# Differential softmax attention beside gated linear attention: finished output tiles copied out of PSUM by ScalarE, and key, weight and input splits reordered

## The chip, the core and the metric

The kernel runs on one core of one Trainium2 chip, as one program. The metric is the device time of an execution in microseconds (us). Engines are called TensorE (PE in the profile; its weight loads are PEld), VectorE (DVE), ScalarE (ACT), GpSimd (POOL) and SyncE (SP, which here only issues transfers).

## What is computed

Two transformer blocks over 1024 tokens of 1024 channels, in fp32. The change lies in the first block's mixer. It has two attentions, whose outputs are joined and multiplied with `w_out`:

```python
o_a = rms_norm(o_fwd + o_bwd) * silu(r_g)            # gated linear attention, 4 heads, both directions
lam = exp(sum(q1*k1)) - exp(sum(q2*k2)) + lambda_init
o_b = diff_attention(qd, kd, vd, positions, rel_bias_table, lam)   # softmax(q1 k1 + bias) - lam * softmax(q2 k2 + bias), times v
o_b = rms_norm(o_b, diff_norm_w) * (1 - lambda_init)  # 4 heads of 128
x = x + g_a * (concatenate([o_a, o_b]) @ w_out)
```

## The kernel before

TensorE multiplies fp32 values as sums of two rounded parts, a high one (`hi`) and a low one (`lo` = value - `hi`): three products, hi*hi, hi*lo and lo*hi. Who makes the two parts is named all through the program: the high part is a copy into the rounded type, the low part a subtraction.

`both_attentions` is one block of the program with an instruction list for each engine. Engines run their lists in order and meet at semaphores.

**Linear part** (`gla_mixer`, about 342 to 393 us). 16 steps, two of them a batch. For step n TensorE makes `scores(n+1)`, `turn` of an older batch on every second step, and `outputs(n)`. ScalarE squares a finished pair of outputs (L2629; the squares themselves are thrown away, into the weight buffer `w_staged`) and takes the root; VectorE masks, carries the states on, scales and gates. `outputs` of a later batch waits for the gate of the one that used its PSUM pair before. After batch 4, ScalarE calls `when_half`, which rounds the keys of head 0.

**Softmax part** (about 388 to 554 us). N = 32 tiles: 4 heads by 8 tiles of 128 queries, each against all 1024 keys. Tile n goes through these steps:

- GpSimd prepares the tile's queries and their two parts (L3070 to L3075). In `KEYS` stands after which tiles it also splits the keys of a head (L3059, L3061); at tiles 8 and 9 it makes the low parts of the two first strips of `w_out` (L3081).
- TensorE: `scores(n)` (L3098), two maps of 128x1024, both softmaxes of the difference.
- VectorE: `add_bias(n)` (L3201, two instructions), then `join(n)` (L3206 to L3212), which subtracts the two maps in the ratio of their sums.
- ScalarE: two `exp` (L3175).
- TensorE: `turn(n)` (L3107), eight transposes of the joined map into PSUM.
- ScalarE: `take_turned(n)` (L3147), copies them to `att_aT`.
- TensorE: `multiply(n)` (L3116), eight products with the values into one of two PSUM places `ps_o[n % 2]`.
- VectorE: `take(n)` (L3217), copies the finished 128x128 output to `att_o`.
- ScalarE: `square(n)` (L3153), for the RMS norm.

The order on each engine is written by hand, as iterations n: TensorE does `scores(n+1)`, `multiply(n-2)`, `turn(n-1)`; VectorE `add_bias(n)`, `take(n-3)`, `join(n-1)`; ScalarE two `exp` of tile n, `take_turned(n-1)`, `square(n-4)`. The waits at the products are these:

```python
def multiply(n):
    h = n // TT
    pe.wait_ge(copied, n + 1)      # take_turned(n)
    if n:
        pe.wait_ge(taken, n)       # take(n - 1)
```

After the last tiles come the norm's factors (`mean`, `root`, `factor`), and for each head `scale` (VectorE, L3242), `turn_head` (TensorE, L3124) and `place` (ScalarE, L3161), which put the head into `mixed`. Then semaphores are cleared, all engines meet at a barrier, and `project("mix")` multiplies `mixed` with `w_out`. There `SplitParts` splits the eight input rows of `mixed`: ScalarE the high parts (L1567 for two halves of row 0, L1571 for the others), VectorE the low ones (L1582, L1586); TensorE's products (L348) follow row by row. The strips of `w_out` for it come through `w_staged`, two of them loaded and split during the softmax part.

Of the kernel before, what the change touches and what calls it, by code (L numbers as in the profile page):

```python
# [20 lines left out]
P = 128  # L21
# [1532 lines left out]
class SplitParts(Part):  # L1554


    def __init__(self, nc, nm, x, kb, hi, lo, halved=False, open_gate=None):
        self.open_gate = open_gate
        self.nc, self.nm, self.x, self.kb, self.hi, self.lo = nc, nm, x, kb, hi, lo
        self.split0, self.half0, self.halved = nm.n_split, nm.n_half_split, halved  # L1560
        nm.n_half_split += halved
# [15 lines left out]
    def vector(self, dve, behind_first=None):  # L1577
        if self.halved:
            for a, ready, at, done in ((0, self.nm.half_high, self.half0 + 1, self.nm.half_split),
                                       (BANK, self.nm.hi_ready, self.split0 + 1, self.nm.split)):  # L1580
                dve.wait_ge(ready, at)
                self.nc.vector.tensor_tensor(self.lo[:, 0, a:a + BANK], self.x[:, 0, a:a + BANK], self.hi[:, 0, a:a + BANK].bitcast(F32),  # L1582
                                             ALU.subtract).then_inc(done, 1)
        for k in range(self.halved, self.kb):
# [990 lines left out]
def gla_mixer(nc, g, ctx, mixed, kd, vtok, qk, fwd, kst_tok, first, psum, junk, att, o_n):  # L2575
# [46 lines left out]
    def scalar(act, when_half):  # L2622
# [13 lines left out]
        for b in range(BATCH):  # L2636
# [3 lines left out]
            if b == BATCH // 2:  # L2640
                when_half(act)
# [7 lines left out]
    def tensor(pe, ahead):  # L2649
# [321 lines left out]
def both_attentions(nc, g, st, mixed, kd, vtok, lam, image_stored, qk, fwd, kst_tok, first, qk_at, fwd_at, q_room_at, states_at):  # L2971
# [5 lines left out]
    KEYS = {0: 0, 3: 1, 5: 2, 7: 3}  # L2977
    base, loads = st.strips, tuple(st.loads)
    with ExitStack() as ctx:
# [9 lines left out]
        junk_of_linear = st.staged[1][:, 0:4 * P].rearrange("p (n c) -> p n c", c=P)  # L2989
        k_rooms = [(qk_at, qk_at + 2 * ROW), (qk_at + ROW, qk_at + 3 * ROW), (fwd_at + ROW, fwd_at + 3 * ROW), (parts_at, parts_at + ROW)]  # L2990
# [7 lines left out]
        e = [[fwd[:, 0, :], fwd[:, 2, :]], [later[:, i, :] for i in range(2)]]  # L2998
        a = [over(f"att_a{s}", [P, L], states_at + s * ROW) for s in range(2)]
        aT = [over(f"att_aT{s}", [P, TT, P], states_at + (2 + s) * ROW) for s in range(2)]  # L3000
        o = over("att_o", [P, N, P], states_at + 4 * ROW)
# [6 lines left out]
        of_linear = gla_mixer(nc, g, ctx, mixed, kd, vtok, qk, fwd, kst_tok, first, psum, junk_of_linear, att, o_n)  # L3008
# [35 lines left out]
        def _(sp):  # L3044
            linear_sync(sp)
            sp.wait_ge(image_stored, 16 * TT * HEADS)
            rows = g.dram["bias"].rearrange("h r k -> (h r) k")
            for n in range(N):
# [3 lines left out]
                if 2 <= n < 4:  # L3052
                    sp.dma_start(st.staged[n - 2][:, :], g.dram["w_out"][n - 2]).then_inc(st.loaded[n - 2], 16)

        @block.gpsimd
        def _(pool):
            def split_keys(h):
                if h:
                    nc.gpsimd.tensor_copy(kd_hi[h][:, :], kd[:, h, :]).then_inc(k_high, 1)  # L3059
# [3 lines left out]
            linear_gpsimd(pool)  # L3063
            linear_loaded(pool)
            linear_updated(pool)
            for n in range(N):
# [10 lines left out]
                if n in KEYS:  # L3077
                    split_keys(KEYS[n])
                if 8 <= n < 10:
                    pool.wait_ge(st.hi_ready, base + n - 7)  # L3080
                    nc.gpsimd.tensor_tensor(st.lo[n - 8][:, :], st.staged[n - 8][:, :], st.hi[n - 8][:, :].bitcast(F32),  # L3081
                                            ALU.subtract).then_inc(st.split, 1)
# [59 lines left out]
        def _(act):  # L3142
# [5 lines left out]

            def square(n):
# [44 lines left out]
        def _(dve):  # L3194
# [20 lines left out]
            def take(n):  # L3215
                dve.wait_ge(summed, n + 1)
# [2464 lines left out]
```

## Time and profile before

| | |
|---|---|
| time, median of 3 executions | 2237.03 us (2232.4 to 2237.46) |
| profiled execution: its time, its span | 2236.17 us, 2234.3 us |
| mean granted clock of TensorE | 0.985 of full speed |
| TensorE busy | 2134.9 us, 96% of the span |
| VectorE busy | 1569.6 us, 70% |
| ScalarE, GpSimd busy | 813.6 us, 36%; 944.4 us, 42% |

The span goes from the first to the last instruction; the profiled execution's own time has 1.9 us around it. Busy times are of the whole program; the change touches the part from 342 to about 580 us, so the table only says that TensorE leads.

### The profile page before, as it was taken

To read this page: it belongs to the slowest core of one execution; us is meant where nothing else is said; L and a number is where in the kernel's file an instruction comes from. 1 tells how busy PE (TensorE), PEld (TensorE's weight loads), DVE (VectorE), ACT (ScalarE), POOL (GpSimd) and SP (SyncE) were. 2 spreads that over 40 slices of the span, in tenths; PEclk is the share of its full clock that TensorE was granted. 3 is DMA by queue.
4 is the path that set the end of the run, shared out by engine and by line. 5 is a ranking of instruction groups with operands and counts; after the bars stand their busy time and mean duration, and the time that the engine had idled before them with its cause. 6 is when DMAs were issued, how large, how long until landed. Compare 5 with 4: busy or idle time off the path is not lost. (4 is left out here: it accounts for less than half of the span.)

```text
span 2234.3 us, 29465 instructions
## 1 busy us (share of the span) xinstructions
PE 2134.9 (96%) x11276; PEld 1735.6 (78%) x11276; DVE 1569.6 (70%) x2298; ACT 813.6 (36%) x1132; POOL 944.4 (42%) x719
## 2 busy tenths in 40 slices
PE   6999999898999999999999999999997999999997
PEld 4887887687877788888777786888877787777876
DVE  5785516997858888888778776869986636764344
ACT  4104432687234344434322224115225323442331
POOL 0222342631435888888656455111000021798710
PEclk9999999999999999999999999899998999999998
DMA  7595732332432333333577764494458323111131
GB/s 275 213 335 162 204 122 96 123 120 69 150 117 76 122 131 131 109 128 110 209 244 244 247 211 169 157 300 132 141 174 288 125 87 118 48 48 48 57 132 75
DMA packets 155431, 337.74 MB, mean 151 GB/s; under 512 B 14039, under 2 KB 92791, under 8 KB 152185
## 3 DMA queue, kind: packets, MB, share of 16 engines
q1 hardware_dynamic: 152292, 330.75, 44.1%
q10 hardware_dynamic: 3000, 5.15, 0.7%
q8 instruction: 88, 1.44, 0.3%
q14 instruction: 51, 0.41, 0.1%
HBM read 259.52 MB, written 93.09 MB: 158 GB/s over the span
## 5 line engine op out<-in xcount | busy, mean ns | idle before, releaser
L282 POOL TENSOR_TENSOR w_lo<-w_staged,w_hi 128x1024 fp32r<-128x1024 f32 x26 | 63.5, 2443 | 378.6 <-ACT w_hi L232 378.5
L2352 POOL TENSOR_TENSOR w_lo<-w_staged,w_hi 128x1024 fp32r<-128x1024 f32 x31 | 80.1, 2583 | 251.8 <-ACT w_hi L2333 251.8
L232 ACT CAST w_hi<-w_staged 128x1024 fp32r<-128x1024 f32 (+1 forms) x33 | 33.8, 1023 | 216.5 <-DMA w_staged<-in_w_u 40.3
L3727 POOL TENSOR_TENSOR w_lo<-w_staged,w_hi 128x512 fp32r<-128x512 f32 x61 | 83.4, 1367 | 61.9 <-ACT w_hi L3723 61.9
L2333 ACT CAST w_hi<-w_staged 128x1024 fp32r<-128x1024 f32 x31 | 32.5, 1049 | 157.9 <-PE ps_in L2361 105.9
L2361 PE MATMUL ps_in<-h_hi,w_hi 128*128 128x512 f32 x272 | 86.9, 400 | 1.0 <-DVE h_lo L1928 1.0
L3723 ACT CAST w_hi<-ff_room 128x512 fp32r<-128x512 f32 x60 | 36.7, 612 | 134.1 <-POOL ff_room L3744 129.3
L2361 PE MATMUL ps_in<-h_lo,w_hi 128*128 128x512 f32 x272 | 85.2, 394 | 0.0
L3431 POOL TENSOR_TENSOR ff_room<-s_par 128x480 f32<-128x480 f32 x32 | 39.1, 1221 | 102.1 <-PE ps_n L3472 52.4
L468 POOL TENSOR_TENSOR w_lo<-w_staged,w_hi 128x512 fp32r<-128x512 f32 x40 | 64.4, 1616 | 21.1 <-ACT w_hi L464 20.9
L3116 PEld LDWEIGHTS ps_attentions<-x_in,att_aT 128*128 128x128 f32 x512 | 59.8, 192 | 13.5 <-issue 10.9
L3116 PE MATMUL ps_attentions<-x_in,att_aT 128*128 128x128 f32 x512 | 65.8, 282 | 2.2 <-ACT att_aT L3147 2.2
L3529 DVE SCALAR_TENSOR_TENSOR mixed<-mixed,cond 128x512 f32<-128x512 f32 x56 | 67.8, 1228 | 0.0
L2361 PE MATMUL ps_in<-h_hi,w_lo 128*128 128x512 f32 x272 | 66.9, 389 | 0.0
L3723 ACT CAST w_hi<-w_staged 128x512 fp32r<-128x512 f32 x80 | 49.7, 622 | 41.1 <-PE ps_next L3761 23.7
L3070 POOL TENSOR_SCALAR kst_tok<-mixed 128x128 f32<-128x128 f32 x32 | 26.0, 814 | 90.1 <-PE ps_attentions L3098 76.8
L2361 PEld LDWEIGHTS ps_in<-h_hi,w_hi 128*128 128x128 f32 x272 | 50.4, 190 | 14.6 <-issue 3.4
L3463 ACT COPY mixed<-ps_n 128x768 f32<-128x768 f32 x16 | 12.8, 800 | 134.3 <-PE ps_n L3455 134.3
L2361 PEld LDWEIGHTS ps_in<-h_lo,w_hi 128*128 128x128 f32 x272 | 51.6, 190 | 11.2
L2361 PEld LDWEIGHTS ps_in<-h_hi,w_lo 128*128 128x128 f32 x272 | 51.1, 188 | 10.7
L3598 DVE SCALAR_TENSOR_TENSOR ada_acc<-ada_w,cond,ada_acc 128x512 f32<-128x512 f32 x56 | 52.1, 930 | 1.8
L3732 DVE TENSOR_TENSOR w_lo<-ff_room,w_hi 128x512 fp32r<-128x512 f32 x39 | 37.7, 966 | 21.6 <-ACT w_hi L3723 21.6
(821 smaller groups left out, 7042.6 us busy)
## 6 DMA issues: line engine op xcount, KB each, us to landing
w_staged<-in_w_ff SPq DMA_DIRECT2D x46, 512.0 KB, 3.6
x_in<-in_w_ada SPq DMA_DIRECT2D x16, 1024.0 KB, 7.2
scratch_bias<-scratch_line SPq DMA_DIRECT2D x32, 512.0 KB, 7.8
kst_tok<-scratch_bias SPq DMA_DIRECT2D x32, 512.0 KB, 3.4
ada_w<-in_w_ada SPq DMA_DIRECT2D x8, 2048.0 KB, 10.8
scratch_x<-x SPq DMA_DIRECT2D x3, 4096.0 KB, 15.0
scratch_ff_a<-mixed SPq DMA_DIRECT2D x22, 512.0 KB, 3.0
ff_raw<-scratch_ff_a SPq DMA_DIRECT2D x20, 512.0 KB, 4.8
```

What stands on the lines that cost most here:

```text
L232: nc.scalar.copy(st.hi[i % 2][:, 0:widths[i]], st.staged[i % 2][:, 0:widths[i]]).then_inc(st.hi_ready, 1)
L282: nc.gpsimd.tensor_tensor(st.lo[i % 2][:, 0:widths[i]], st.staged[i % 2][:, 0:widths[i]], st.hi[i % 2][:, 0:widths[i]].bitcast(F32), ALU.s ...
L468: self.nc.gpsimd.tensor_tensor(self.slot(self.st.lo, q, m), self.weights[m], self.slot(self.st.hi, q, m).bitcast(F32), ALU.subtract).then_ ...
L2352: nc.gpsimd.tensor_tensor(st.lo[i % 2][:, :], st.staged[i % 2][:, :], st.hi[i % 2][:, :].bitcast(F32), ALU.subtract).then_inc(st.split, 1)
L2361: last = nc.tensor.matmul(ps[i % 2][:, a:a + BANK], u[i % 2][:, k * P:(k + 1) * P], r[:, k, a:a + BANK], start=(k == 0 and part == 0), sto ...
L3116: last = nc.tensor.matmul(ps_o[n % 2], aT[n % 2][:, k, :], vtok[:, k, HEADS + h, :], start=(k == 0), stop=(k == TT - 1))
L3431: v.tensor_tensor(out, wide(xa), stretched(ya), ALU.mult).then_inc(self.by_pool, 1)
L3529: v.scalar_tensor_tensor(acc, here, by, acc, ALU.mult, ALU.add).then_inc(self.weighted, 1)
L3598: v.scalar_tensor_tensor(acc, here, by, acc, ALU.mult, ALU.add).then_inc(self.weighted, 1)
L3723: self.nc.scalar.copy(self.slot(self.st.hi, q, m), self.weights[m]).then_inc(self.high_ready, 1)
L3727: self.nc.gpsimd.tensor_tensor(self.slot(self.st.lo, q, m), self.weights[m], self.slot(self.st.hi, q, m).bitcast(F32), ALU.subtract).then_ ...
L3732: self.nc.vector.tensor_tensor(self.slot(self.st.lo, q, m), self.weights[m], self.slot(self.st.hi, q, m).bitcast(F32), ALU.subtract).then_ ...
```

## The change

- ScalarE makes the copy `take(n-3)`, in its iteration n, between the two `exp` of tile n and `take_turned(n-1)`. VectorE's copy is gone.
- Keys: the high parts of heads 0 and 1 are made by ScalarE beside linear batches 4 and 5, their low parts by GpSimd ahead of the softmax loop. Heads 2 and 3 get their high parts from GpSimd after tiles 3 and 9, their low parts from VectorE two iterations later.
- Strips of `w_out`: loaded first of all in the block, high parts by ScalarE after linear batches 1 and 2, low parts by GpSimd ahead of the loop. The squares of the linear part are thrown away into PSUM, since `w_staged` is now in use.
- Linear part: `outputs(n)` goes ahead of `turn((n-3)//2)` on TensorE.
- Input rows 0 and 1 of the next stage: high parts by GpSimd behind the loop, low parts by VectorE as the last thing in the block; `SplitParts` begins with row 2 (`ready=2`), and its halves of row 0 are gone.
- Some buffers lie elsewhere, so that these tiles are free at that time.

```diff
@@ class SplitParts
-        if self.halved:
-            for a, done in ((0, self.nm.half_high), (BANK, self.nm.hi_ready)):
-                self.nc.scalar.copy(self.hi[:, 0, a:a + BANK], self.x[:, 0, a:a + BANK]).then_inc(done, 1)
-        for k in range(self.halved, self.kb):
+        for k in range(self.ready, self.kb):
...
@@ gla_mixer, scalar
-                nc.scalar.activation(junk[:, 2 * (n % 2) + h, :], ps_o[n // 2 % 2][:, h, (n % 2) * P:(n % 2 + 1) * P], ACT.Square,
+                bank = ps_o[n // 2 % 2][:, h, :]
+                nc.scalar.activation(bank[:, (2 + n % 2) * P:(3 + n % 2) * P], bank[:, (n % 2) * P:(n % 2 + 1) * P], ACT.Square,
...
-            if b == BATCH // 2:
-                when_half(act)
+            beside(act, b)
@@ gla_mixer, tensor
+            outputs(n)
             if n >= 3 and n % 2:
                 turn((n - 3) // 2)
-            outputs(n)
@@ both_attentions
-    KEYS = {0: 0, 3: 1, 5: 2, 7: 3}
+    KEYS = {3: 2, 9: 3}
+    EARLY = 2
+    STRIPS_AT = (1, 2)
...
@@ both_attentions, sync
+            for i in range(2):
+                sp.dma_start(st.staged[i][:, :], g.dram["w_out"][i]).then_inc(st.loaded[i], 16)
             linear_sync(sp)
...
-                if 2 <= n < 4:
-                    sp.dma_start(st.staged[n - 2][:, :], g.dram["w_out"][n - 2]).then_inc(st.loaded[n - 2], 16)
@@ both_attentions, gpsimd
             linear_gpsimd(pool)
+            for i in range(2):
+                pool.wait_ge(st.hi_ready, base + i + 1)
+                nc.gpsimd.tensor_tensor(st.lo[i][:, :], st.staged[i][:, :], st.hi[i][:, :].bitcast(F32), ALU.subtract).then_inc(st.split, 1)
             linear_loaded(pool)
+            for h in range(EARLY):
+                low_keys(h)
             linear_updated(pool)
...
                 if n in KEYS:
-                    split_keys(KEYS[n])
-                if 8 <= n < 10:
...
+                    nc.gpsimd.tensor_copy(kd_hi[KEYS[n]][:, :], kd[:, KEYS[n], :]).then_inc(k_high, 1)
+
+            pool.wait_ge(turned, N)
+            pool.wait_ge(summed, N - 1)
+            for k in range(2):
+                nc.gpsimd.tensor_copy(f_hi[:, k, :], mixed[:, k, :]).then_inc(nm.hi_ready, 1)
@@ both_attentions, scalar
+            def take(n):
+                act.wait_ge(summed, n + 1)
+                nc.scalar.copy(o[:, n, :], ps_o[n % 2]).then_inc(taken, 1)
...
+            def beside_linear(act, b):
+                if b in STRIPS_AT:
+                    i = STRIPS_AT.index(b)
+                    act.wait_ge(st.loaded[i], loads[i] + 16)
+                    nc.scalar.copy(st.hi[i][:, :], st.staged[i][:, :]).then_inc(st.hi_ready, 1)
+                if b == TT // 2:
+                    linear_loaded(act)
+                if 0 <= b - TT // 2 < EARLY:
+                    h = b - TT // 2
+                    nc.scalar.copy(kd_hi[h][:, :], kd[:, h, :]).then_inc(k_high, 1)
...
             for n in range(N + 4):
                 if n < N:
...
                 if n == N:
                     root(0)
+                if 3 <= n < N + 3:
+                    take(n - 3)
                 if 1 <= n <= N:
                     take_turned(n - 1)
                 if n == N + 2:
                     place(0)
-                if 4 <= n < 6:
-                    act.wait_ge(st.loaded[n - 4], loads[n - 4] + 16)
-                    nc.scalar.copy(st.hi[n - 4][:, :], st.staged[n - 4][:, :]).then_inc(st.hi_ready, 1)
                 if n >= 4:
                     square(n - 4)
@@ both_attentions, vector
-            def take(n):
-                dve.wait_ge(summed, n + 1)
-                nc.vector.tensor_copy(o[:, n, :], ps_o[n % 2]).then_inc(taken, 1)
+            def low_keys(h):
+                dve.wait_ge(k_high, h + 1)
+                nc.vector.tensor_tensor(kd_lo[h][:, :], kd[:, h, :], kd_hi[h][:, :].bitcast(F32), ALU.subtract).then_inc(k_split, 1)
...
                 if 0 < n < N:
                     add_bias(n)
-                if n >= 3:
-                    take(n - 3)
+                if n - 2 in KEYS:
+                    low_keys(KEYS[n - 2])
...
             scale(HEADS - 1)
+            for k in range(2):
+                dve.wait_ge(nm.hi_ready, split0 + k + 1)
+                nc.vector.tensor_tensor(f_lo[:, k, :], mixed[:, k, :], f_hi[:, k, :].bitcast(F32), ALU.subtract).then_inc(nm.split, 1)
@@ build
-            split = SplitParts(nc, nm, mixed, KD, hi, lo, halved=True)
+            split = SplitParts(nc, nm, mixed, KD, hi, lo, ready=2)
```

## Rows read from the trace of the kernel before

**Rows 1.** Windows: length; busy of PE, PEld, DVE, ACT, POOL; clock, DMA share, GB/s.
```profile
409.00:537.00 128.00, 125.25 (x1007) 103.94 (x1003) 120.60 (x226) 101.93 (x196) 52.53 (x83) 1.00 0.34 111
537.00:554.00 17.00, 11.75 (x96) 10.60 (x96) 9.94 (x23) 12.26 (x25) 0.00 (x0) 1.00 0.00 1
554.00:563.00 9.00, 6.13 (x15) 4.87 (x16) 6.80 (x7) 7.64 (x10) 0.00 (x0) 0.62 0.72 252
```

**Rows 2.** Timeline of ScalarE, one softmax step: start, length, engine, line, operation.
```profile
...
464.75 1.01 ACT L3147 COPY att_aT<-ps_attentions 128x1024 f32<-128x1024 f32 x1 [0.91 <-PE ps_attentions L3107]
465.66 0.31 ACT L3153 ACTIVATE kst_tok<-att_o 128x128 f32<-128x128 f32 x1
...
465.96 1.14 ACT L3175 ACTIVATE att_s<-att_s,att_low 128x1024 f32<-128x1024 f32 x1
...
467.10 1.14 ACT L3175 ACTIVATE att_s<-att_s,att_low 128x1024 f32<-128x1024 f32 x1
```

**Rows 3.** Timeline of TensorE's weight loads, the same step.
```profile
...
461.79 1.86 PEld L3116 LDWEIGHTS ps_attentions<-x_in,att_aT 128*128 128x128 f32 x16 [0.36 <-issue]
463.57 0.91 PEld L3107 LDWEIGHTS ps_attentions<-consts,att_a 128*128 128x128 f32 x8
...
466.24 1.86 PEld L3116 LDWEIGHTS ps_attentions<-x_in,att_aT 128*128 128x128 f32 x16 [0.36 <-issue]
```

**Rows 4.** Timeline of ScalarE: first exp of tiles 3 and 31, a table load.
```profile
...
409.35 1.15 ACT L3175 ACTIVATE att_s<-att_s,att_low 128x1024 f32<-128x1024 f32 x1
...
537.14 1.14 ACT L3175 ACTIVATE att_s<-att_s,att_low 128x1024 f32<-128x1024 f32 x1
...
541.29 1.28 ACT L3157 ACT_TABLE_LOAD   x1
```

**Rows 5.** Groups by line, VectorE, 409 to 537 us: count, busy, mean ns.
```profile
...
L3212 DVE SCALAR_TENSOR_TENSOR att_a<-qk_fwd,att_ratio 128x1024 f32<-128x1024 f32 x15 | 19.4, 1291 | 0.5
L3217 DVE COPY att_o<-ps_attentions 128x128 f32<-128x128 f32 x28 | 8.0, 286 | 0.0
```

**Rows 6.** Groups by line, ScalarE, 382 to 391 us.
```profile
...
L2629 ACT ACTIVATE w_staged<-ps_attentions 128x128 f32<-128x128 f32 x8 | 2.1, 278 | 7.0 <-PE ps_attentions L2683 7.0
```

**Rows 7.** Timeline of both engines: a copy, and the weight load that waits for it.
```profile
...
539.96 1.01 ACT L3147 COPY att_aT<-ps_attentions 128x1024 f32<-128x1024 f32 x1 [0.45 <-PE ps_attentions L3107]
...
541.02 1.86 PEld L3116 LDWEIGHTS ps_attentions<-x_in,att_aT 128*128 128x128 f32 x16 [1.34 <-ACT att_aT L3147]
```

**Rows 8.** Windows behind two holes of TensorE.
```profile
402.00:406.00 4.00, 3.64 (x16) 2.78 (x17) 3.62 (x8) 3.27 (x5) 0.65 (x3) 0.57 0.40 128
702.00:707.00 5.00, 4.77 (x14) 3.77 (x15) 5.00 (x3) 1.90 (x4) 3.66 (x2) 0.66 0.40 120
```

**Rows 9.** Timeline of TensorE: the first matmuls behind these holes.
```profile
400.86 0.88 PE L3107 MATMUL ps_attentions<-consts,att_a 128*128 128x128 f32 x6 [2.68 <-DVE att_a L3212]
...
702.23 0.50 PE L3761 MATMUL ps_up<-f_hi,w_hi 128*128 128x512 f32 x1 [2.15 <-DVE mixed L4270]
```

**Rows 10.** Timeline of all engines around the loop's start.
```profile
...
386.64 0.66 PE L2691 MATMUL ps_attentions<-consts,gla_on 128*128 128x128 f32 x4 [0.62 <-DVE gla_on L2726]
...
390.48 0.53 POOL L3070 TENSOR_SCALAR kst_tok<-mixed 128x128 f32<-128x128 f32 x1 [10.54 <-PE ps_attentions L3098]
...
397.33 2.39 POOL L3061 TENSOR_TENSOR att_k_lo<-kd,att_k_hi 128x1024 fp32r<-128x1024 f32 x1
...
397.53 3.28 DVE L3212 SCALAR_TENSOR_TENSOR att_a<-qk_fwd,att_ratio 128x1024 f32<-128x1024 f32 x1
```

**Rows 11.** Timeline of all engines from the last scaling to the next stage.
```profile
...
550.50 1.22 DVE L3242 TENSOR_TENSOR att_o<-att_o,att_fac 128x1024 f32<-128x1024 f32 x1
...
552.91 1.11 ACT L3161 ACTIVATE mixed<-ps_attentions,vecs 128x1024 f32<-128x1024 f32 x1 [1.54 <-PE ps_attentions L3124]
...
555.38 1.14 ACT L1567 CAST f_hi<-mixed 128x512 fp32r<-128x512 f32 x2 [1.36 <-PEq L5355]
...
556.87 0.76 PE L348 MATMUL ps_mix<-f_hi,w_hi 128*128 128x512 f32 x1 [4.00 <-DVE f_lo L1582]
```

More of the change, by code:

```diff
@@ L1577, in vector @@
     def vector(self, dve, behind_first=None):
[L1578 to L1584, printed above, removed]
+        for k in range(self.ready, self.kb):
             dve.wait_ge(self.nm.hi_ready, self.split0 + k + 1)
@@ L2572, in projections, with gla_mixer @@
     st.loads = [loads[0] + 16 * ((n + 1) // 2), loads[1] + 16 * (n // 2)]
-def gla_mixer(nc, g, ctx, mixed, kd, vtok, qk, fwd, kst_tok, first, psum, junk, att, o_n):
+def gla_mixer(nc, g, ctx, mixed, kd, vtok, qk, fwd, kst_tok, first, psum, att, o_n):
     STEPS = 2 * TT
@@ L2620, in sync, with scalar @@
         back(mixed[:, 7:8, :], 7, 1, qd_loaded)
-    def scalar(act, when_half):
+    def scalar(act, beside):
         def square(n):
@@ L2968, in vector, with both_attentions @@
                                                ALU.mult, ALU.add).then_inc(by_dve, 1)
-def both_attentions(nc, g, st, mixed, kd, vtok, lam, image_stored, qk, fwd, kst_tok, first, qk_at, fwd_at, q_room_at, states_at):
+def both_attentions(nc, g, st, mixed, kd, vtok, lam, image_stored, qk, fwd, kst_tok, first, qk_at, fwd_at, q_room_at, states_at, f_hi, f_lo):
     N = HEADS * TT
-    KEYS = {0: 0, 3: 1, 5: 2, 7: 3}
+    KEYS = {3: 2, 9: 3}
+    EARLY = 2
+    STRIPS_AT = (1, 2)
     base, loads = st.strips, tuple(st.loads)
@@ L2997, in both_attentions @@
         later = tile("att_s1", [P, 2, L])
[L2998 to L3001, printed above, removed]
+        e = [[qk[:, 1, :], qk[:, 3, :]], [later[:, i, :] for i in range(2)]]
+        o = over("att_o", [P, N, P], states_at)
+        a = [over(f"att_a{s}", [P, L], states_at + (4 + s) * ROW) for s in range(2)]
+        aT = [over(f"att_aT{s}", [P, TT, P], states_at + (6 + s) * ROW) for s in range(2)]
+        nm, split0 = st.nm, st.nm.n_split
         low, total = (tile(f"att_{n}", [P, N, 2]) for n in ("low", "total"))
@@ L3007, in both_attentions @@
         ps_o = [ps_out[:, s * P:(s + 1) * P] for s in range(2)]
-        of_linear = gla_mixer(nc, g, ctx, mixed, kd, vtok, qk, fwd, kst_tok, first, psum, junk_of_linear, att, o_n)
+        of_linear = gla_mixer(nc, g, ctx, mixed, kd, vtok, qk, fwd, kst_tok, first, psum, att, o_n)
         linear_sync, linear_scalar, linear_gpsimd, linear_tensor, linear_vector, linear_loaded, linear_updated, linear_done = of_linear
@@ L5349, in build @@
             tile(attending, "gla_states_room", [P, KD, L])
-            both_attentions(nc, g, st, mixed, kd, vtok, lam[:, :], image_stored, qk, fwd, kst_tok, first, qk_at, fwd_at, q_room_at, states_at)
+            ahead_at = hi_at + 4 * (KD * L + 2 * whole_lines(TT) + whole_lines(NPAR))
+            f_hi, f_lo = (nc.alloc_sbuf_tensor_at(name, [P, KD, L], F32R, offset=ahead_at + 4 * KD * L * i) for i, name in enumerate(("f_hi", "f_lo")))
+            both_attentions(nc, g, st, mixed, kd, vtok, lam[:, :], image_stored, qk, fwd, kst_tok, first, qk_at, fwd_at, q_room_at, states_at, f_hi, f_lo)
         linear.close()
@@ L5367, in build @@
         f_at = nc._sbuf_addr_for_side("left")
-        hi, lo = tile(normed, "f_hi", [P, KD, L], F32R), tile(normed, "f_lo", [P, KD, L], F32R)
+        assert f_at == ahead_at
+        tile(normed, "f_room", [P, 2 * KD, L])
+        hi, lo = f_hi, f_lo
         with ExitStack() as ctx:
-            split = SplitParts(nc, nm, mixed, KD, hi, lo, halved=True)
+            split = SplitParts(nc, nm, mixed, KD, hi, lo, ready=2)
             norm = SplitHalvesKept(nc, g, nm, st, normed, "n2", x, vec("ffn_norm"), mod(SC_F, 0), mod(SH_F, 0), hi, lo, rms, mixed[:, :, :])
```

22 lines of the change are left out of this document (6 added, 16 removed).

## The prediction

> **What bounds the kernel now.** I read the page first: TensorE is busy for 96% of the span and VectorE for 70% (the table above has them). That share says little about the change, which touches about 215 of 2234 us, so the stretches come next [rows 1]. In the softmax attention's steady part, 409 to 537 us, TensorE is busy 125 of 128 us and VectorE 121; ScalarE is busy 102. In the stretch from the last softmax tile to the next stage TensorE has holes, and its mean clock just after is 0.62 of full speed.
>
> Then the timeline of one step. ScalarE goes through `exp` twice, waits about 0.9 us for the transposes, copies them to `att_aT`, squares an older tile, and begins the next `exp` at once [rows 2]. TensorE's weight loads show multiply (461.79), transposes (463.57) and the next multiply (466.24) [rows 3]; the scores lie between. One multiply to the next is 4.45 us. So a step costs 4.45 us by TensorE; VectorE, busy 121 of 128 us, is at 4.3. Over all 28 steps from tile 3's `exp` (409.35) to tile 31's (537.14) the mean is 127.8 / 28 = 4.56 us [rows 4].
>
> For each new wait I ask which instruction stands ahead of it on its engine, and whether that instruction waits in turn for what the wait holds up.
>
> **The copy of finished outputs.** It moves 32 copies of 128x128 out of PSUM, 0.29 us each, from VectorE [rows 5] to ScalarE. What that gives VectorE is small: its step falls from 4.3 to 4.0, but TensorE's is 4.45. At most the mean 4.56 falls to 4.45, 3 us in 28 steps.
>
> Its place is what counts. Write E(n) for the two `exp` of tile n, K for `take`, M for `multiply`, T for `turn`, C for `take_turned`, Q for `square`. ScalarE's iteration n is E(n), K(n-3), C(n-1), Q(n-4). TensorE's is scores(n+1), M(n-2), T(n-1). `multiply(n)` waits for `taken >= n`, so M(n-2) needs K(n-3). Until now VectorE made that copy between its bias additions of tile n and the join; in the changed kernel it stands behind E(n). The loop is then closed, and it advances by one tile only:
>
> E(n), K(n-3), M(n-2), T(n-1), C(n-1), Q(n-4), E(n+1).
>
> Each waits for the one ahead of it, by the order of its engine or by a semaphore. In the trace M of the same iteration begins at 466.24, while the second `exp` begins at 467.10 and frees ScalarE 1.14 later, at 468.24 [rows 2, 3]. So M would be late by over 2 us on every step. The terms of one turn of the loop:
>
> - E(n) to K: an `exp` holds ScalarE for 1.14 (465.96 to 467.10) until its next instruction [rows 2]; two of them 2.28.
> - K: not in the trace on ScalarE. The nearest row is a square of a 128x128 tile read from PSUM, 0.28 [rows 6]; above it is 0.31, the square from SBUF [rows 2]. Below I allow 0.1, since the copy has no accumulator to read. I take 0.28.
> - K to M: 0.05, as from the end of a copy (539.96 + 1.01) to the weight load that waits for it at 541.02 [rows 7].
> - M to T 1.78 (461.79 to 463.57) and T to C 1.18 (463.57 to 464.75) [rows 2, 3].
> - C to Q 0.91 and Q to E(n+1) 0.30 [rows 2].
>
> Sum 6.78 us a step. VectorE (4.0) and GpSimd are covered by that, and scores and the join run inside it. There are 28 such steps, the first without a square (0.3 less): 28 x (6.78 - 4.56) - 0.3 = +61.9 us. An error of 0.15 us in the sum is 4 us.
>
> The Trainium skill (TensorE: Matmul & The Clock Gate, section Architectural detail) says that TensorE may pull weight loads ahead of matmuls in flight, while ScalarE and VectorE are strictly first in, first out. If ScalarE could pass the copy ahead of the `exp`, the result would be the first rival's 2227 us; by the rule it is the forecast. Nothing shown here has an instruction overtake another on ScalarE.
>
> **TensorE's clock inside the new step.** TensorE works 4.45 of 6.78 us, with one hole of 2.3 us. A hole of 2.68 us ended at 400.86, and from 402 to 406 the clock was 0.57, so 4 x 0.43 = 1.7 us of speed were lost [rows 8, 9]. Behind a hole of 2.15 us, which ended at 702.23, the clock of 5 us is 0.66, most of it at the low level of 1.2 GHz [rows 8, 9]. From 537 to 554 TensorE was busy 11.75 of 17 us, 0.69, at full clock [rows 1]; the new step has 0.66. Bounds: nothing, and 28 x 1.7 = 48 us. By the share of work the long row at full clock is nearest, by the length of the hole the two others; I take 3 us, two low stretches.
>
> **The early keys and weights, and the start of the loop.** High and low keys of heads 0 and 1 and the low halves of the two strips go ahead of the loop, onto ScalarE (four casts, about 1.0 us like the `att_aT` copy [rows 2]) and GpSimd (four subtractions of 2.39 us [rows 10]). There ScalarE waits 7.0 us in front of two batches of squares [rows 6], and GpSimd idles 10.5 us ahead of tile 2's queries [rows 10], so I cost them at nothing; without that cover they would be 9.6 us of GpSimd. Their two loads go first in SP's queue, ahead of the keys, which nobody reads before batch 4. Gone is a collision: the join of tile 0 took 3.28 us beside GpSimd's subtraction [rows 10], against a mean of 1.29 later [rows 5]. That makes E(2) 2.0 us earlier; the slow clock's part of the next step (at most 1.7) gives 1.1 more. So tile 3's `exp` begins 3.1 us earlier; bounds 0 and 5. The later collisions are inside the 4.56 that the new loop replaces. Low keys 2 and 3 cost VectorE 1.2 us each, in 2.5 us of slack.
>
> **Linear outputs ahead of the turn.** In the last batch TensorE waited 0.62 us in front of the turn and 0.66 in it [rows 10]; the outputs now go first, up to 1.2 us gained. In the earlier batches the gate comes behind a later turn, and only the next scores cover it, which are about as long: some 0.3 for each of six, an estimate, 1.8 lost. Squares now go into PSUM, at the same price. I take 0; bounds -1 and +3.
>
> **The tail.** Now place(3), L3161's last, ends 16.9 us after E(31) began (537.14 to 554.02) [rows 4, 11]. In the new order, counted from E(31): K(28) 2.3, M(29) 2.6, T(30) 4.4, C(30) 5.6, Q(27) 6.5, the table load (1.28 [rows 4]) and root to 8.4, K(29), M(30) 8.7, C(31) 11.7, Q(28), K(30) 13.0, M(31) 13.35, K(31) 15.5, place(0), Q(30), Q(31), place(1) to 18.8, root, factor, scale(3) 19.5, then from scale(3) to the end of place(3) 3.5 as now (550.50 to 554.02) [rows 11]: 23.0. That is +6.0 to +6.1; I take 6.0.
>
> **Two input rows split early.** After the barrier ScalarE began f_hi at 555.38, and the first product began at 556.87 [rows 11]. With rows 0 and 1 ready it can begin at about 555.4: -1.5. The low halves (2 x 1.22 on VectorE, the length of scale(3) [rows 11], and behind it) end 0.15 after place(3): +0.15. GpSimd's two casts (about 1.0 each) are made while C(31) and M(31) run. From row 2 on, the splits (1.2 us a row) stay ahead of the products. The hole before the products goes from 4.0 [rows 11] to 2.5 us; whether the clock still falls is open, 2 us either way.
>
> The Trainium skill (SBUF — State Buffer, section Terms) says of the port pair that GpSimd and VectorE share that the loser "fully blocks" for the whole instruction. By it the two casts could hold scale(1) or scale(2) by up to 2.1 us. An estimate from that page: it would fit within the 2 us by which scale(2) precedes M(31)'s end, and the sum stays.
>
> **Sum.** 61.9 - 3.1 + 0 + 6.0 - 1.35 + 3 = +66.45. The profiled execution took 2236.2 us (span 2234.3 and 1.9 around it), 0.9 under the median, 2237.0. So 2302.6 beside the profiled execution, and about 2303 beside the median.
>
> **The rivals.**
> 1. *Faster: the copy is made in time.* M does not wait for a copy behind the same iteration's `exp`, because there is slack that I overlooked. Then VectorE's relief counts: -3.1 (start), -3.1 (4.56 to 4.45), -1.35 (early rows), and about -1.5 in the tail: -9, 2227 us. It decides if K ends before M's natural start, 2 us earlier than the rows allow. ScalarE has 0.9 us free in a step, which speaks for it; but that time lies behind the `exp`, where it comes too late. Chance 0.05.
> 2. *The clock falls on most steps.* Then each hole is followed by 1.7 us of lost speed in M and T, both in the loop: up to 48 us instead of 3, 2348 us; half of the steps give 2324. The holes of 2.15 and 2.68 us speak for it, the stretch busy for 0.69 against. Chance 0.10 for over 2318.
> 3. *The change does nothing measurable,* because the longer step is made up elsewhere: nothing behind the attention waits for a clock time, and no 60 us of idle TensorE exist to absorb it. Chance 0.01, 2237 us.
> 4. *The forecast:* the loop closes at 6.5 to 7.0 us a step, with few falls of the clock. Chance 0.84; its own range is 2290 to 2316.
>
> **How the numbers follow.** No change is within 0.3%, 6.7 us, about what this measurement can tell. Faster 0.05, same 0.01, slower 0.94. The range takes in the forecast's, the bounds of the start, the linear part and the end (together -7 to +6 us), and the lighter half of rival 2: 2286 to 2328.
>
> **What would show it.** In the changed kernel's timeline M begins 0.05 us after ScalarE's 128x128 copy, in every step; from one first `exp` to that of the next tile is 6.8 us; TensorE's wait in front of M, with ScalarE's `att_o` as its releaser, sums to 60 us or more; VectorE's share in the loop drops from 0.94 [rows 1] to about 0.6. The clock column in the loop shows rival 2. The prediction fails if M begins ahead of that copy, or if the two `exp` don't stand ahead of it on ScalarE.

## The result and the profile after

The changed kernel takes 2306.1 us in the median of 4 executions (2300.7 to 2309.2), the kernel before 2236.6: a ratio of 1.031, with a 95% interval from 1.029 to 1.033. It is slower, by 69.5 us. The forecast was 2303 us, with a range from 2286 to 2328. The profiled execution took 2303.1 us, and the rest of this section is about it.

The page of the changed kernel: TensorE's work is the same, its share of the longer span is not.

```profile
span 2301.3 us, 29464 instructions
...
PE 2135.5 (93%) x11276; PEld 1737.0 (75%) x11276; DVE 1556.2 (68%) x2267; ACT 816.7 (35%) x1162; POOL 932.0 (40%) x718
...
```

The timeline of one softmax step of the changed kernel (start, length, engine, line, operation, what ended the idle time before it):

```profile
...
481.05 1.14 ACT L3182 ACTIVATE qk<-qk,att_low 128x1024 f32<-128x1024 f32 x1
...
482.18 1.14 ACT L3182 ACTIVATE qk<-qk,att_low 128x1024 f32<-128x1024 f32 x1
...
483.31 0.25 ACT L3147 COPY att_o<-ps_attentions 128x128 f32<-128x128 f32 x1
483.67 1.86 PEld L3112 LDWEIGHTS ps_attentions<-x_in,att_aT 128*128 128x128 f32 x16 [2.72 <-issue]
483.70 2.02 PE L3112 MATMUL ps_attentions<-x_in,att_aT 128*128 128x128 f32 x16 [2.31 <-ACT att_o L3147]
...
485.45 0.91 PEld L3103 LDWEIGHTS ps_attentions<-consts,att_a 128*128 128x128 f32 x8
...
486.64 1.01 ACT L3143 COPY att_aT<-ps_attentions 128x1024 f32<-128x1024 f32 x1 [3.08 <-PE ps_attentions L3103]
...
487.55 0.32 ACT L3153 ACTIVATE kst_tok<-att_o 128x128 f32<-128x128 f32 x1
...
487.85 1.14 ACT L3182 ACTIVATE att_s<-att_s,att_low 128x1024 f32<-128x1024 f32 x1
...
```

Read it along the loop that the prediction wrote down. ScalarE makes two `exp` (481.05, 482.18), then the 128x128 copy (483.31). TensorE's weight load for the multiply begins at 483.67. Its matmuls stood idle for 2.31 us, and the releaser named is ScalarE's copy to `att_o`. The transposes follow at 485.45, the copy of the transposed map at 486.64, the square at 487.55, the next tile's `exp` at 487.85. One turn is 6.80 us. In the kernel before the multiply began ahead of the same iteration's second `exp` [rows 2, 3].

The tile view of `att_o` in the changed kernel sums this wait (us, times):

```profile
...
L3147 ACT COPY att_o<-ps_attentions x32: 243/247/266, 408.8 to 616.2; 128x128 f32<-128x128 f32 x32
...
who waited for it (us, times):
  PE ps_attentions L3112: 72.2, 31
...
```

Windows of the changed kernel (busy us of PE, PEld, DVE, ACT, POOL, then granted clock, DMA share, GB/s):

```profile
...
409.00:598.00 189.00, 123.96 (x996) 103.61 (x996) 112.53 (x200) 102.85 (x221) 32.86 (x76) 1.00 0.22 73
598.00:620.00 22.00, 14.84 (x88) 13.85 (x88) 7.08 (x15) 9.70 (x24) 2.02 (x2) 0.77 0.00 0
620.00:630.00 10.00, 6.38 (x22) 5.07 (x23) 7.53 (x7) 6.76 (x8) 0.00 (x0) 0.66 0.42 138
...
```

The first answers to the first of [rows 1]: TensorE's work in the steps is the same, 124 us against 125, now spread over 189 us instead of 128. VectorE's share falls from 0.94 to 0.60. The other two windows have mean clocks of 0.77 and 0.66.

ScalarE's timeline around the loop's two ends (tiles 0, 3 and 31, the first `exp` of each), which answers to [rows 4]:

```profile
...
392.95 1.15 ACT L3182 ACTIVATE qk<-qk,att_low 128x1024 f32<-128x1024 f32 x1 [0.66 <-DVE att_low L3207]
...
406.51 1.15 ACT L3182 ACTIVATE att_s<-att_s,att_low 128x1024 f32<-128x1024 f32 x1
...
```

```profile
...
596.67 1.14 ACT L3182 ACTIVATE att_s<-att_s,att_low 128x1024 f32<-128x1024 f32 x1
...
```

28 steps take 596.67 - 406.51 = 190.2 us, 6.79 each, against 4.56 [rows 4]. With the first product of the linear part and that of the next stage the span can be divided as follows; each line is a difference between two rows of one trace:

| stretch | before | changed | difference | forecast |
|---|---|---|---|---|
| start of the program to the linear part's first product | 342.81 | 342.24 | -0.6 | 0 |
| to tile 0's first `exp` | 49.81 | 50.71 | +0.9 | 0 |
| to tile 3's first `exp` | 16.73 | 13.56 | -3.2 | -3.1 |
| 28 steps, to tile 31's first `exp` | 127.79 | 190.16 | +62.4 | +61.9 and the clock's 3 |
| to the next stage's first product | 19.73 | 28.05 | +8.3 | +4.65 |
| to the end of the span | 1677.4 | 1676.6 | -0.8 | 0 |
| sum | 2234.3 | 2301.3 | +67.0 | +66.45 |

### The profile page after: what moved, and what is told of

Read it like the earlier page. It is cut to its first block and busy times, and to the rows that moved or that the text cites. A ratio compares the mean times of both kernels' runs of the same rounds, so it can differ in the third digit from the quotient of the medians.

```text
span 2301.3 us, 29464 instructions
## 1 busy us (share of the span) xinstructions
PE 2135.5 (93%) x11276; PEld 1737.0 (75%) x11276; DVE 1556.2 (68%) x2267; ACT 816.7 (35%) x1162; POOL 932.0 (40%) x718
## 5 line engine op out<-in xcount | busy, mean ns | idle before, releaser
L3065 POOL TENSOR_SCALAR kst_tok<-mixed 128x128 f32<-128x128 f32 x32 | 17.4, 545 | 146.2 <-PE ps_attentions L3094 146.2
L3143 ACT COPY att_aT<-ps_attentions 128x1024 f32<-128x1024 f32 x32 | 32.5, 1015 | 100.1 <-PE ps_attentions L3103 100.1
L3207 DVE CUSTOM_DVE_ANT_0 att_s<-ps_attentions,kst_tok 128x1024 f32<-128x1024 f32 x32 | 37.9, 1223 | 38.7 <-PE ps_attentions L3094 38.5
L3207 DVE CUSTOM_DVE_ANT_0 qk<-ps_attentions,kst_tok 128x1024 f32<-128x1024 f32 x32 | 37.9, 1222 | 33.8 <-PE ps_attentions L3094 33.6
L2351 PEld LDWEIGHTS ps_in<-h_hi,w_hi 128*128 128x128 f32 x272 | 49.8, 188 | 14.4 <-issue 3.4
```

The source lines that it names most:

```text
L2351: last = nc.tensor.matmul(ps[i % 2][:, a:a + BANK], u[i % 2][:, k * P:(k + 1) * P], r[:, k, a:a + BANK], start=(k == 0 and part == 0), sto ...
L3207: nc.vector.tensor_tensor_reduce(e[n % 2][i], score_map(n, i), bias[n % 2], 1.0, 3.0e38, ALU.add, ALU.min, low[:, n, i:i + 1]).then_inc(bi ...
```

## The experiments

Theory A is the prediction's: the copy behind the `exp` closes a loop, and whatever ScalarE does between C and K counts in full. Rival B says that the copies cost ScalarE too much, or that one of the other edits is at fault. Rival C puts the holes and the loss down to TensorE's clock.

| run | edit | us, median | ratio to before, 95% | mean step |
|---|---|---|---|---|
| changed kernel | | 2306.1 | 1.029 to 1.033 | 6.79 |
| e1_ahead | copy ahead of both `exp` | 2235.4 | 0.997 to 1.001 | 4.55 |
| e2_between | copy between them | 2274.0 | 1.014 to 1.020 | 5.66 |
| e3_alone | kernel before, this copy only | 2316.4 | 1.033 to 1.039 | 7.03 |
| e4_rest | changed, copy on VectorE | 2232.9 | 0.997 to 1.000 | 4.51 |
| e5_behind_turned | copy right behind C | 2232.6 | 0.997 to 0.999 | 4.46 |
| e6_turn_first | e4, linear turn first again | 2228.6, one execution | | 4.52 |
| e7_square_early | changed, square in the wait | 2309.0 | 1.030 to 1.033 | 6.86 |
| e8_changed_again | none | 2307.9, one execution | | 6.84 |
| e9_combined | e5 and turn first | 2231.1 | 0.997 to 0.999 | 4.46 |
| e10_copy_alone_placed | kernel before, copy right behind C | 2237.0 | 0.999 to 1.002 | 4.55 |

The mean step is from tile 3's first `exp` to tile 31's, over 28. The kernel before is at 2236 to 2237 us with 4.56. The total carries noise from parts that no edit touches: from the next stage's first product to the end the changed kernel took 1676.6 us in its first profile and 1678.9 in its second (e8).

### Where the copy stands (e1, e2)

```diff
@@ e1_ahead, ScalarE's iteration n
+                if 3 <= n < N + 3:
+                    take(n - 3)
                 if n < N:
                     for i in range(2):
...
-                if 3 <= n < N + 3:
-                    take(n - 3)
```

> The changed kernel with one edit: ScalarE makes take(n-3) at the head of its iteration n, ahead of the two exp of tile n. Theory A (the copy closes a loop E, K, M, T, C, Q that advances by one tile, and each of them counts): M no longer waits for the same iteration's exp, the step goes back from 6.79 to TensorE's 4.45 to 4.5 us, TensorE's wait for att_o (72 us in all) is gone, time 2224 to 2232 us. Rival B (ScalarE is too slow for the copies, or another edit of the change costs the 67 us): the copies are still ScalarE's and all other edits stay, so the time stays above 2290 us. Rival C (the hole comes from TensorE's clock): as B, since nothing of the clock is touched.

```diff
@@ e2_between
                         nc.scalar.activation(e[n % 2][i], e[n % 2][i], ACT.Exp, scale=-1.0, bias=low[:, n, i:i + 1],
                                              accum_out=total[:, n, i:i + 1]).then_inc(exped, 1)
+                        if i == 0 and n >= 3:
+                            take(n - 3)
...
-                if 3 <= n < N + 3:
+                if N <= n < N + 3:
                     take(n - 3)
```

> The changed kernel with the copy between the two exp of tile n, instead of behind them. Theory A: one exp, 1.13 us, leaves the loop and runs beside M: the step is 6.79 - 1.13 = 5.66 us, 28 steps save 32 us, and with the same tail the time is 2271 to 2276 us, clearly between both. If a copy on ScalarE costs by itself, or if any other edit is the cause (B), it stays at 2306. If only 'late or not' counts, and not by how much, it is either 2306 or about 2228.

Both keep the copies on ScalarE and all other edits, so rival B wanted over 2290 us from either. e2 lands on its forecast: 2274.0 us, step 5.66. One `exp` out of the loop is 1.13 us off every step. So a delay counts by its length, and "late or not" is not what decides. Rival C would have left both runs at 2306 us, since neither touches the clock; and in the changed kernel the clock of the steps was 1.00 (window 409 to 598 above).

e1 took 2235.4 us, which is 70.7 us off the changed kernel, but 3 us above its forecast. The step is 4.55 and not 4.45. Its timeline (ScalarE and TensorE's matmuls, two steps):

```profile
...
471.42 0.26 ACT L3147 COPY att_o<-ps_attentions 128x128 f32<-128x128 f32 x1
471.57 1.16 ACT L3184 ACTIVATE att_s<-att_s,att_low 128x1024 f32<-128x1024 f32 x1
...
471.82 2.02 PE L3112 MATMUL ps_attentions<-x_in,att_aT 128*128 128x128 f32 x16
...
473.68 1.04 PE L3103 MATMUL ps_attentions<-consts,att_a 128*128 128x128 f32 x8
...
474.76 1.02 ACT L3143 COPY att_aT<-ps_attentions 128x1024 f32<-128x1024 f32 x1 [0.81 <-PE ps_attentions L3103]
...
475.67 0.31 ACT L3153 ACTIVATE kst_tok<-att_o 128x128 f32<-128x128 f32 x1
...
475.97 0.26 ACT L3147 COPY att_o<-ps_attentions 128x128 f32<-128x128 f32 x1
...
476.37 2.02 PE L3112 MATMUL ps_attentions<-x_in,att_aT 128*128 128x128 f32 x16
...
```

Two multiplies begin 4.55 us apart, and no idle time is written ahead of them. But a second loop is closed here, without the `exp`: multiply 471.82, transposes 473.68, copy 474.76, square 475.67, output copy 475.97, multiply 476.37. That is 1.86 + 1.08 + 0.91 + 0.30 + 0.40 = 4.55. It lies just above TensorE's 4.45. e5 tests that.

### One part alone, and the rest without it (e3, e4)

```diff
@@ e3_alone: the kernel before
@@ ScalarE
                     root(0)
+                if 3 <= n < N + 3:
+                    take(n - 3)
@@ VectorE
-                if n >= 3:
-                    take(n - 3)
```

> The kernel before with this one part of the change alone: the copy on ScalarE behind the two exp, everything else as it was (keys, strips, linear order, early rows). Theory A: start as before (tile 3's exp at 409), 28 steps of 6.79 instead of 4.56 give +62, the tail +6 to +10: 2304 to 2309 us. Rival B (the loss is in the reordered keys, strips or rows): at most 2245 us.

e4_rest is the counterpart, all of the change but the copy's move:

```diff
@@ e4_rest: the changed kernel, ScalarE
-                if 3 <= n < N + 3:
-                    take(n - 3)
@@ VectorE
                 if 0 < n < N:
                     add_bias(n)
+                if n >= 3:
+                    take(n - 3)
```

> The changed kernel with the copy back on VectorE in its old place; all other edits of the change stay. Theory A: what the other edits give by themselves: start 2.8 us earlier, first products 1.3 us earlier, fewer collisions of GpSimd and VectorE inside the loop (mean step 4.56 to about 4.47, 2.6 us): 2228 to 2232 us. Rival B: above 2290 us.

The copy alone costs all that the change lost, and more: 2316.4 us. The rest alone takes 2232.9. That settles rival B: nothing of the loss is in the keys, strips, rows or the linear order. e4 is 0.9 us above its forecast, with a step of 4.51 where 4.47 was expected; the section on e10 comes back to it.

e3 is 7 us above its forecast of 2304 to 2309. Steps that aren't disturbed take 6.80 there too, but five of the 28 take 7.75 to 8.42. In three of these (8.16, 8.42 and 8.24) the clock is at its low level for a part. In the other two, 7.76 and 7.75, it is at full speed; e3 still has the kernel before's casts of the strips on ScalarE, and they stand in the loop, between the copy of the transposed map and the square:

```profile
...
423.60 1.02 ACT L3147 COPY att_aT<-ps_attentions 128x1024 f32<-128x1024 f32 x1 [3.08 <-PE ps_attentions L3107]
424.51 1.05 ACT L3191 CAST w_hi<-w_staged 128x1024 fp32r<-128x1024 f32 x1
425.45 0.31 ACT L3157 ACTIVATE kst_tok<-att_o 128x128 f32<-128x128 f32 x1
...
```

The cast puts off the square by 425.45 - 424.51 = 0.94 us, and 6.80 + 0.94 = 7.74: whatever ScalarE does between C and K counts in full, as theory A says. The two casts and the three low stretches add 6.6 us to e3's 28 steps.

### The second loop (e5)

```diff
@@ e5_behind_turned: the changed kernel, ScalarE
-                if 3 <= n < N + 3:
-                    take(n - 3)
                 if 1 <= n <= N:
                     take_turned(n - 1)
+                if 2 <= n < N + 2:
+                    take(n - 2)
```

> The changed kernel with the copy directly behind take_turned: in its iteration n ScalarE makes the two exp, take_turned(n-1), take(n-2), square(n-4). It is the copy one iteration earlier than in the changed kernel. Where the copy stands ahead of the exp, behind the square, the step was 4.55 us and not TensorE's 4.45. Theory A says why: another loop, M, T, C, Q, K, M, with 1.86 + 1.08 + 0.91 + 0.30 + 0.40 = 4.55 us. With the copy directly behind C the square's 0.30 leaves it: 4.25, under TensorE's 4.45. So the step is 4.44 to 4.46 us and the first product of the next stage 2 to 4 us earlier than with the copy ahead of the exp; total 2229 to 2234 us. If the 0.10 came from something else (PSUM reads that slow each other, clock), the step stays at 4.55.

The step is 4.46 in the mean, 4.44 to 4.46 in the undisturbed ones. From tile 3's `exp` to tile 31's it takes 125.0 us, where e1 took 127.4. The square was in e1's loop, and it is out of this one. From the linear part's first product to the next stage's, e5 is 2.0 us shorter than e1. The windows of e5 show who sets the step now:

```profile
...
409.00:532.00 123.00, 121.75 (x986) 102.14 (x984) 112.31 (x199) 102.34 (x219) 35.43 (x77) 1.00 0.34 112
...
```

TensorE is busy 121.75 of 123 us.

### TensorE's clock inside the steps (e7, e8)

```diff
@@ e7_square_early
                 if 3 <= n < N + 3:
                     take(n - 3)
+                if 4 <= n < N + 3:
+                    square(n - 4)
                 if 1 <= n <= N:
                     take_turned(n - 1)
...
-                if n >= 4:
+                if n >= N + 3:
                     square(n - 4)
```

> The changed kernel with only the square moved: behind the copy, ahead of take_turned, in the 3.1 us in which ScalarE waits for M and T. The work of every engine is the same. Theory A: the square's 0.30 us leaves the loop, the step is 6.80 - 0.30 = 6.50 us, 28 steps save 8.5 us: 2295 to 2300 us. If the step were set by ScalarE's amount of work, or by TensorE's clock, nothing would change: 2306.

> The changed kernel once more, unaltered, for the clock. In its first profile the clock fell three times between 599 and 625 us and not once in the 28 steps; with the copy alone in the kernel before it fell three times inside the steps as well (8.2 instead of 6.8 us each). Theory: a hole of 2.3 us lowers the clock or not by chance of its place, so a second profile has the steps without a fall at 6.80 again and may have steps of about 8.2; total 2300 to 2312. If the falls belong to the other kernel's order, no step is longer than 6.9.

e7 is the instructive miss. The step is as forecast, 6.51 us. Yet the kernel is no faster: 2309.0 us. ScalarE's timeline in e7, first `exp` of three tiles and the copy of a transposed map:

```profile
...
429.67 1.15 ACT L3182 ACTIVATE qk<-qk,att_low 128x1024 f32<-128x1024 f32 x1
...
436.90 1.02 ACT L3143 COPY att_aT<-ps_attentions 128x1024 f32<-128x1024 f32 x1 [4.40 <-PE ps_attentions L3103]
437.81 1.15 ACT L3182 ACTIVATE att_s<-att_s,att_low 128x1024 f32<-128x1024 f32 x1
...
444.32 1.15 ACT L3182 ACTIVATE qk<-qk,att_low 128x1024 f32<-128x1024 f32 x1
...
```

One step is 437.81 - 429.67 = 8.14 us, the next 444.32 - 437.81 = 6.51. The windows show why (the columns as above):

```profile
...
425.00:432.00 7.00, 4.48 (x36) 3.74 (x36) 4.45 (x10) 4.22 (x11) 1.78 (x5) 1.00 0.25 77
432.00:439.00 7.00, 6.11 (x36) 5.36 (x36) 2.82 (x6) 2.60 (x8) 1.27 (x2) 0.76 0.24 76
439.00:446.00 7.00, 4.49 (x36) 3.74 (x36) 4.44 (x8) 4.22 (x10) 1.65 (x5) 1.00 0.24 75
...
```

The same work of TensorE takes 6.11 us instead of 4.48, and the mean clock is 0.76. In e7 six of the 28 steps are like this, from the second one on every fifth. Six times 1.62 is 9.7 us, and about 28 x 0.29 = 8.1 had been saved. It was not this profile alone: the mean clock of e7's four executions was 0.976 to 0.980, that of the changed kernel's four 0.982 to 0.985. The changed kernel had none of 28 in its first profile and one in the second (8.24 us, e8), so the falls do not belong to the other kernel's order. The hole of 2.0 to 2.3 us in every step is there in all three. So whether the clock falls is not a matter of the hole's length alone; what else decides it no run here shows. Rival 2's mechanism is real, though it decided little in the changed kernel.

### The other edits, and a combination (e6, e9, e10)

```diff
@@ e6_turn_first (on e4_rest), and the same on e5 for e9_combined
             if n + 1 < STEPS:
                 scores(n + 1)
-            outputs(n)
             if n >= 3 and n % 2:
                 turn((n - 3) // 2)
+            outputs(n)
```

> The changed kernel with the copy on VectorE and, besides, the linear part's turn ahead of the outputs again, as before the change. It prices that reorder by itself: tile 0's exp began at 392.6 before the change and at 393.1 with all edits but the copy. If the reorder costs those 0.5 us (the gate comes behind a later turn), tile 0's exp goes back to 392.6 or a little earlier; if it gains up to 1.2 us as its last batch suggests, tile 0's exp goes to 394 or later. Total within 1 us of the run without this edit, which a time can't tell.

That expectation counted from the start of the program. It should not have: in e6 the linear part itself began 3.3 us earlier than in e4 (339.15 us against 342.40), and it did so too in e10 (339.18), whose program is the kernel before's up to there. From the linear part's first product to tile 0's `exp` it is 50.3 us in e6, 50.7 in e4 and in the changed kernel, 49.8 in the kernel before. So the reorder costs 0.4 us, and by difference the early keys and strips together with the squares into PSUM another 0.5. e6's total is 4.3 us below e4's, where 1 us had been expected; 3.3 of it lie ahead of the linear part, where the two programs are the same. The wait that the reorder makes can be seen in VectorE's groups by line, 343 to 388 us. In the changed kernel:

```profile
...
L2725 DVE TENSOR_TENSOR mixed<-ps_attentions,mixed 128x512 f32<-128x512 f32 x6 | 4.2, 692 | 6.1 <-PE ps_attentions L2681 6.1
...
```

and in the kernel before:

```profile
...
L2735 DVE TENSOR_TENSOR mixed<-ps_attentions,mixed 128x512 f32<-128x512 f32 x7 | 4.8, 686 | 0.7 <-PE ps_attentions L2691 0.7
...
```

The gate waits 6.1 us for the transposes instead of 0.7. Since the whole stretch grew by only 0.9 us, most of that is hidden.

> The changed kernel with the copy directly behind take_turned and the linear part's turn ahead of the outputs again. The run with the copy behind take_turned had a step of 4.46 us in the mean and 50.7 us from the linear part's first product to tile 0's exp; with the turn first that stretch was 50.3, and 49.8 in the kernel before. Expected: 50.3 and 4.46 again, the first product of the next stage 0.4 us earlier counted from the linear part's start, total 2229 to 2234 us, faster than before by 0.1 to 0.3%. Rival: the two edits meet (ScalarE's square waits for outputs, and the order of both is new), then the stretch stays at 50.7.

e9 is faster than the kernel before by 0.2%: 2231.1 us, ratio 0.998 with an interval from 0.997 to 0.999, as e5's is. The stretch was 50.2 us and the step 4.46, both as expected. Whether e9 beats e5 can't be told from the times.

e10_copy_alone_placed has e5's place for the copy and nothing else of the change:

```diff
@@ e10_copy_alone_placed: the kernel before, ScalarE
                 if 1 <= n <= N:
                     take_turned(n - 1)
+                if 2 <= n < N + 2:
+                    take(n - 2)
@@ VectorE
-                if n >= 3:
-                    take(n - 3)
```

> The kernel before with only the copy moved to ScalarE, directly behind take_turned, nothing else of the change. It prices VectorE's relief by itself. Theory A: TensorE sets 4.45 us of the step, so VectorE's 0.2 to 0.3 us return little: the 28 steps go from 127.8 to between 124.6 (all at 4.45) and 127.8, and the total from 2237 to 2233 to 2237. If VectorE had been the bound, a step would fall to 4.2 us, 10 us in all: 2227.

It changes nothing: 2237.0 us, and the 28 steps take 127.5 us instead of 127.8. In the kernel before, VectorE's relief by itself is worth no more than that, since TensorE sets most steps.

With the rest of the change it is worth more. The 28 steps take 126.4 and 126.6 us with the copy on VectorE (e4, e6), and 125.0 in both runs with it behind C (e5, e9). The difference lies in the steps behind VectorE's two subtractions of keys: 5.08 and 5.27 us in e4, 4.61 and 4.46 in e5. VectorE's timelines behind the first of them show how fast it catches up, in e4 and then in e5:

```profile
...
418.00 1.22 DVE L3201 CUSTOM_DVE_ANT_0 qk<-ps_attentions,kst_tok 128x1024 f32<-128x1024 f32 x1 [0.17 <-DVE att_a L3212]
...
422.40 1.22 DVE L3201 CUSTOM_DVE_ANT_0 att_s<-ps_attentions,kst_tok 128x1024 f32<-128x1024 f32 x1 [0.17 <-DVE att_a L3212]
...
```

```profile
...
417.75 1.22 DVE L3207 CUSTOM_DVE_ANT_0 qk<-ps_attentions,kst_tok 128x1024 f32<-128x1024 f32 x1 [0.17 <-DVE att_a L3218]
...
421.95 1.22 DVE L3207 CUSTOM_DVE_ANT_0 att_s<-ps_attentions,kst_tok 128x1024 f32<-128x1024 f32 x1 [0.17 <-DVE att_a L3218]
...
```

One turn of VectorE takes 4.40 us with the copy and 4.20 without it. TensorE's is 4.45, so VectorE makes up 0.05 us a step in the one and 0.25 in the other, after a delay of 1.1 us. That the delay is what lengthens the two steps is my reading; no run moved these subtractions alone.

## Why the prediction was right

**The loop.** Its terms are measured in the step shown above: `exp` to copy 2.26 (forecast 2.28), copy to multiply 0.36 (0.28 + 0.05), multiply to transposes 1.78 (1.78), transposes to copy 1.19 (1.18), copy to square 0.91 (0.91), square to `exp` 0.30 (0.30). The sum is 6.80, forecast 6.78. The copy itself takes 0.25 us, shorter than the square that stood in for it, and the way from its end to the weight load is 0.11, longer than the 0.05 taken from `att_aT`. e2 and e7 take known lengths out of the loop and the step follows; e3 and e4 show that the whole loss comes with this copy. VectorE's turn was read too low, as its busy time over 28 steps, 4.3 and without the copy 4.0, where the timelines have 4.40 and 4.20; in a step of 6.8 that is covered either way.

**The start.** -3.2 us, forecast -3.1. The join of tile 0 no longer stands beside a subtraction of GpSimd; it took 1.28 us in the changed kernel, 3.28 before [rows 10].

**The linear part.** +0.9, forecast 0 within -1 and +3. By e6 and e4 0.4 of it is the reorder, where the gain expected in the last batch did not outweigh the waits in the earlier ones; the other 0.5 had been priced at nothing.

**The tail and the early rows.** +8.3, forecast +4.65. The timeline from tile 31 on, changed kernel:

```profile
...
598.93 0.25 ACT L3147 COPY att_o<-ps_attentions 128x128 f32<-128x128 f32 x1
...
599.30 3.49 PEld L3112 LDWEIGHTS ps_attentions<-x_in,att_aT 128*128 128x128 f32 x16 [4.11 <-issue]
...
602.66 1.72 PEld L3103 LDWEIGHTS ps_attentions<-consts,att_a 128*128 128x128 f32 x8
...
604.82 1.01 ACT L3143 COPY att_aT<-ps_attentions 128x1024 f32<-128x1024 f32 x1 [5.64 <-PE ps_attentions L3103]
...
607.94 2.76 PEld L3112 LDWEIGHTS ps_attentions<-x_in,att_aT 128*128 128x128 f32 x16 [3.55 <-issue]
...
610.57 1.70 PEld L3103 LDWEIGHTS ps_attentions<-consts,att_a 128*128 128x128 f32 x8
...
612.55 1.01 ACT L3143 COPY att_aT<-ps_attentions 128x1024 f32<-128x1024 f32 x1 [4.72 <-PE ps_attentions L3103]
...
619.65 1.23 DVE L3248 TENSOR_TENSOR att_o<-att_o,att_fac 128x1024 f32<-128x1024 f32 x1
...
622.07 1.11 ACT L3161 ACTIVATE mixed<-ps_attentions,vecs 128x1024 f32<-128x1024 f32 x1 [1.88 <-PE ps_attentions L3120]
...
624.72 1.19 PE L348 MATMUL ps_mix<-f_hi,w_hi 128*128 128x512 f32 x2 [2.69 <-PEq L5366]
...
```

The multiply at 599.30 is followed by the transposes 3.36 us later (1.78 at full clock) and by the copy 2.16 us after that (1.18): 2.6 us lost to the clock. Another low stretch meets the next multiply and its transposes (607.94, 610.57, 612.55), which lose another 1.6 by the same reckoning; the mean clock of 598 to 620 us is 0.77. Without these 4.2 us the tail and early rows are +4.1. The early rows did what was forecast: from the last `place` to the first product there are 624.72 - 622.07 = 2.65 us instead of 3.96 [rows 11].

**The clock.** The prediction put 3 us for it into the 28 steps and nothing into the tail's sum, only 2 us either way for its end. In the steps nothing was lost, which left them 2.5 us under their forecast; in the tail 4.2 us were lost, which left it 3.7 over. That the profiled total lies within 1 us of the forecast is luck to this extent. e3 and e7 lost 4.7 and 9.7 us inside the steps beside holes of the same kind, and rows 8 and 9 could not say which would be the case.

**The rivals.** "Made in time" is refuted by the 2.31 us ahead of every multiply. That rival's world is what e1 and e5 measured, 2235 and 2233 us, where 2227 had been given. In e1 a second loop is in the way. In e5 two of its terms came as given, the start with -3.0 (-3.1) and the steps with -2.8 (-3.1). What it had wrong is the part from tile 31's `exp` to the next stage, 20.4 us against 19.7 before, +0.7 where -2.85 was given, and the linear part's +0.9. Why that part did not shrink stays open; in e5 the clock was at 0.50 from 549 to 554 us, and the next stage began at 552.54. Of rival 2, over 2318 us, the changed kernel showed none of the 28 steps at the low clock in one profile and one in the other. Rival 3, no change, is out by 67 us.

**Order on ScalarE, and the port pair.** In the step above the copy stands behind both `exp`, and it does so in each of the 28. That agrees with the Trainium skill (TensorE: Matmul & The Clock Gate, section Architectural detail), by which ScalarE keeps strictly to the order of its queue. Whether GpSimd's two casts would hold up VectorE at the tail, as the Trainium skill has it for the port pair (SBUF — State Buffer, section Terms), was not put to the test: they ran from 612.58 to 614.60, and VectorE had nothing to do from 611.75 to 618.11:

```profile
...
608.26 3.50 DVE L3248 TENSOR_TENSOR att_o<-att_o,att_fac 128x1024 f32<-128x1024 f32 x3
...
612.58 2.02 POOL L3078 CAST f_hi<-mixed 128x1024 fp32r<-128x1024 f32 x2 [34.45 <-PE ps_attentions L3103]
...
618.11 0.20 DVE L3228 RECIPROCAL att_inv<-att_total 128x8 f32<-128x8 f32 x1 [6.36 <-ACT kst_tok L3153]
...
```

## What to carry to other kernels

When a copy moves to another engine, ask first what stands ahead of it in the new queue and write down the loop that this closes; its length over the number of tiles by which it advances is a lower bound on the step, whatever the engines' busy shares are. Put such a copy where what it waits for is already done, here right behind the copy of the transposed map, and not behind work of a newer tile. And price a relief by the engine that sets the step: VectorE's was worth 0.3 us over 28 steps by itself and 1.4 where VectorE had keys to split as well, while the place of one 0.25 us copy was worth 70 us.

## What the runs showed of the hardware that I had not expected

- With a hole of 2.0 to 2.3 us in every step, TensorE's clock fell in none (changed kernel), one (e8), three (e3) or six (e7) of 28 steps. In e7 this made a step that was 0.29 us shorter worth nothing.
- A low stretch that meets multiply and transposes, which are in the loop here, costs about 1.6 us a step (8.14 against 6.51).
- ScalarE's 128x128 copy out of PSUM took 0.25 us (0.27 in e5) where VectorE's took 0.29 [rows 5], and 0.36 to 0.40 us passed from its start to the multiply that waited for it.
- The kernel before and e10 are the same program up to the linear part, and e10 reached it 3.6 us earlier (339.18 us against 342.81). An absolute time of a row is not to be compared across runs; a stretch between two rows of one trace can be, if the clock is the same in it: from the linear part's first product to tile 0's `exp` the changed kernel, e1, e2, e4, e5, e7 and e8, which share that part, took 50.69 to 50.71 us.
